# The opening of a fused decoder step: states and gate blocks in turn, and an expert loop whose next gate steps run before the combinations

## Chip, core and metric

The kernel runs on one core of one Trainium2 chip. The metric is the device time of one execution in microseconds (us), and smaller is better. TensorE is called PE here, VectorE DVE, ScalarE ACT, GpSimd POOL and SyncE SP.

## What is computed

One layer of a decoder for 256 prompt tokens and 8 sample tokens (264 in all), width 1024, all in float32. Cut to what matters:

```python
h = rmsnorm(x, g_mix); z = h @ w_in              # w_in is 1024 x 7168
q, f, v, g, u, gate_a, gate_b = split(z)
o, S_new = hgrn2(q, 1 - f, v, log f, S0)         # 8 heads of 128x128; the 8 samples carry a state each:
#   S = f * S0 + k (outer) v                     #   one step of it for a sample
merged = sigmoid(gate_a) * rmsnorm(o) * silu(g) + sigmoid(gate_b) * pool_mixer(u)
x = x + merged @ w_out
# experts: top 4 of 32 for each token
gate = min(h2 @ w_gate[e] + b_gate[e], 7); up = clip(h2 @ w_up[e] + b_up[e], -7, 7)
x = x + weight * (((up + 1) * gate * sigmoid(1.702 * gate)) @ w_down[e] + b_down[e])
x = x + sigmoid(rmsnorm(x) @ w_ple_gate) * (p @ w_ple_proj)
y = rmsnorm(x)
```

The outputs are y, the new states and the new pooling rows. Each of the 32 experts has three weight matrices of 4 MB, 384 MB in all, each read once.

## The kernel before

**The front.** The columns of w_in are loaded by SP in 14 chunks of 512 columns (L423) into four slots; the load of a chunk waits for the last use of the slot. PE turns the rows of x (L645), multiplies all chunks block by block (a block is 8 matmuls, `turned_blocks`, L703), and writes each block into a PSUM bank that it may use again only once ACT or DVE have drained the block before it there. The order is q and f (L741), v, the product of the sample queries with the old states (L764), eight blocks of the output gate g (`gT`, banks 0 to 3 twice), four blocks of gate_a (`gaT`, the same banks), scores, and so on. Beside this ACT and DVE make the new states of the eight samples. For a sample b ACT issues a DMA that spreads the sample's values over all partitions (`spread_values`, L1423, 512 KB, into one of three buffers), and multiplies the old state by f (`decay`, L1428, 8 instructions); DVE adds k times v (`new_state`, L1737, 8 instructions), and POOL stores the new state. A gate block is drained by a sigmoid on ACT (L1405) and a product on DVE (L1705). Both engines do four samples, then gate blocks 0 to 3, then four samples, then gate blocks 4 to 7. Later the pooled rows are multiplied by w_pool (`ypT`, L870), the merged rows by w_out (L891, L915), and the router chooses experts.

**The weights of the experts.** They come in granules of 1 MB, `at_` by number: a pair of experts takes 24 granules, 8 each for gate, up and down (two experts in turn). A step of a product (`products`, L1135) uses two granules, one for each expert: 8 matmuls of 512 columns. There are 16 places in a ring (`gran`) and three more places for single granules at the start (`early`). SP issues the loads in order; each waits until the counter `s_used` has reached a number. In the front the counter comes to 8 at the first `ypT` matmul, to 12 at the first matmul by w_out, to 18 at the turning of the last tile of x (L933); after that it rises by one for each granule used. `load_first` (L439, L437 for `early`) loads the first two pairs, `load_experts` (L445) the others.

**The expert loop.** `pair` handles two experts, 16 pairs in all; the first two are written out. On PE a pair is: four bias matmuls, four gate steps, four up steps, gathering of the first half of the next pair's rows (L1043), a wait for the activation that DVE makes (L2005, L2011), turning it (L1061), four down steps, gathering of the second half (L1043, L1053), and then the combinations (`mix`, L1190) that put the results back into the tokens' rows. In pair 0 PE also turns the router weights (L1000), and multiplies the down biases (L1012, L1020) and turns the embeddings (L1029) between its up steps.

Of the kernel before, what the change touches and what calls it, by code (L numbers as in the profile page):

```python
# [14 lines left out]
P = 128  # L15
# [94 lines left out]
def build(nc, x_prompt, x_sample, p_prompt, p_sample, state_hgrn, state_pool, g_mix, w_in,  # L110
# [14 lines left out]
    with ExitStack() as ctx:  # L125
# [61 lines left out]
        def heads(start):  # L187
# [36 lines left out]
        early = {0: view(TMP, GRAN).rearrange("p (j n) -> p j n", j=2),  # L224
                 1: view(V + D, GRAN).rearrange("p (j n) -> p j n", j=2),
# [183 lines left out]
        def place_of(at_):  # L409
            return (at_ + 1) % RING if at_ <= 17 else at_ % RING  # L410
# [5 lines left out]
        def _(sp):  # L416
# [217 lines left out]
        def _(pe):  # L634
# [88 lines left out]
            pe.wait_ge(s_const, 1)  # L723
            for t, half in ((0, 0), (0, 1), (1, 0), (1, 1), (2, 0)):
                pe.wait_ge(s_rows, t + 1)
                turn_half_rows("hT", htok, t, half)
                if (t, half) == (0, 0):
# [3 lines left out]
                    fill_done(pe.transpose(bank[7][:, 0:32], lgin[0:32, :], ident[0:32, 0:32]), ("lb",))  # L731
            wait_turned("hT")
# [344 lines left out]
            def pair(i0, n, opening=False, last=False, project_tiles=False):  # L1077
# [3 lines left out]
                def granules(m, g):  # L1081

                    for one in range(2):
# [4 lines left out]
                        elif isinstance(i0, int) and i0 == 0:  # L1088
                            place = place_of(at_)
                            pe.wait_ge(s_gr[place], 16 if at_ <= 17 else 16 * ((at_ - 19) // RING + 2))  # L1090
# [5 lines left out]
                def products(m, out, src, first):  # L1096

                    for g in range(4):
# [47 lines left out]
                pe.wait_ge(s_esel, i + 1)  # L1146
# [4 lines left out]
                else:  # L1151
                    pe.wait_ge(s_xe, 2 * i + 1)
                    pe.wait_ge(s_free23, i + 1)
                for r in range(4):
                    rows = slice(r * NE, (r + 1) * NE)
                    pe.matmul((GATE + UP)[r][:, :], esel[rows], bias_gu[rows], start=True, stop=False,  # L1156
                              tile_position=(r * NE, 0))
                if opening:
                    pe.wait_ge(s_xe, 1)
                for m, (out, done) in enumerate(((GATE, s_gate), (UP, s_up))):  # L1160
                    products(m, out, xT_e, False).then_inc(done, 1)
# [4 lines left out]
                else:  # L1166
                    if opening:
                        wait_drained(pe, ("pT", 1))
                    pe.wait_ge(s_oh, i + 2)
                    gather(range(4), s_used)  # L1170
                pe.wait_ge(s_actr, i + 1)
                pe.wait_ge(s_free45, i + 1)
                if project_tiles:
                    wait_drained(pe, ("pp", 1, 1))
                for c in range(2):
# [7 lines left out]
                if not last:  # L1183
                    gather(range(4, KD), s_used)
                    gather_samples()
# [27 lines left out]
                else:  # L1213
                    pe.wait_ge(s_ys, 2 * i + 2)
                    mix(0)
# [80 lines left out]
            pair(0, 1)  # L1296
# [6 lines left out]
            with pe.If(more > 0):  # L1303
# [4 lines left out]
                with pe.Fori(1, NBLK) as b:  # L1308
                    with pe.Fori(0, PAIRS // PER) as q:
                        for n in range(PER):  # L1310
                            pair(b * PAIRS + PER * q, n)
# [10 lines left out]
        def _(act):  # L1322
# [820 lines left out]
```

## Time and profile before

| what | value |
| --- | --- |
| time, median of 3 runs | 1289.98 us (1287.83 to 1291.11) |
| the profiled execution: its own time | 1288.42 us |
| its span from the first to the last instruction | 1286.7 us |
| PE busy | 1213.5 us, 94% |
| DVE, ACT, POOL busy | 339.9, 170.2, 48.6 us |
| moved by DMA | 460.98 MB, mean 358 GB/s over the span |
| mean granted TensorE clock | 0.995 |

The measured time is 1.7 us longer than the span. PE's busy time counts instructions, and in the expert loop the time in which one waits for its operand is partly hidden in the gaps between them, so 94% is not a statement of what bounds the kernel.

### The profile page before, as it was taken

How to read it: one execution, taken by the hardware profiler on the slowest of the kernel's cores; microseconds unless marked ns; L12 is line 12 of the kernel's file. 1: busy time of each engine (PE TensorE's matmuls, PEld its weight loads, DVE VectorE, ACT ScalarE, POOL GpSimd, SP SyncE). 2: the span in 40 equal slices, each digit the busy share in tenths (PEclk: the TensorE clock that was granted, in tenths of full speed). 3: DMA queues.
4: the chain of work that ended last, by engine and by line, in shares of the span. 5: the costliest groups of instructions: out<-in, count | busy, mean ns of one | idle time of the engine just before them, and what ended most of it. 6: DMA issues, size and time to landing. Idle time of an engine off the chain costs nothing.

```text
span 1286.7 us, 15777 instructions
## 1 busy us (share of the span) xinstructions
PE 1213.5 (94%) x6296; PEld 597.6 (46%) x6296; DVE 339.9 (26%) x685; ACT 170.2 (13%) x434; POOL 48.6 (4%) x129
## 2 busy tenths in 40 slices
PE   7999899999999999999898998989898989899996
PEld 6857788856333343333334243333333333434244
DVE  3154434534312222112121121211121212112224
ACT  3135113111100100001010000000010101001013
POOL 2221100010000000000000000000000000000001
PEclk9999999999999999999999999999999999999999
DMA  9847621497989999999999999999999999999971
GB/s 342 285 144 243 243 107 47 180 381 300 418 356 423 421 420 422 422 422 423 422 422 421 422 421 423 422 422 422 422 422 422 422 422 422 422 421 421 422 287 36
DMA packets 79782, 460.98 MB, mean 358 GB/s; under 512 B 8158, under 2 KB 9235, under 8 KB 30842
## 3 DMA queue, kind: packets, MB, share of 16 engines
q1 hardware_dynamic: 74512, 445.18, 84.7%
q0 software_dynamic: 3280, 10.75, 2.6%
q10 hardware_dynamic: 1946, 4.43, 1.0%
q8 instruction: 31, 0.51, 0.2%
q14 instruction: 13, 0.11, 0.0%
HBM read 454.41 MB, written 6.39 MB: 358 GB/s over the span
## 4 chain that ended last, share of the span: by engine, by line
PE 73%; DMA 23%; DVE 3%; issue 1%; SPq 0%; ACT 0%; POOLq 0%; POOL 0%; DVEq 0%; ACTq 0%
PE bank L1135 37%; DMA arena<-in_w_down_dram 19%; PE bank L703 7%; PE bank L1190 5%; PE bank L741 4%; PE bank L1043 3%; DMA arena<-in_w_up_dram 2%; PE bank L684 2%; DMA arena<-sample_values 1%; PE bank L1053 1%; PE bank L1245 1%; PE bank L1156 1%; DVE arena L1737 1%; PE bank L1263 1%; PE bank L891 1%; PE bank L915 1%
## 5 line engine op out<-in xcount | busy, mean ns | idle before, releaser
L1135 PE MATMUL bank<-arena 128*64 128x512 f32 x3072 | 677.1, 595 | 37.0 <-DMA arena<-in_w_up_dram 25.1
L1135 PEld LDWEIGHTS bank<-arena 128*64 128x64 f32 x3072 | 221.4, 137 | 474.1 <-issue 468.9
L703 PE MATMUL bank<-arena 128*128 128x264 f32 x512 | 117.9, 391 | 6.7 <-DVE arena L1705 6.7
L703 PEld LDWEIGHTS bank<-arena 128*128 128x128 f32 x512 | 97.7, 193 | 24.6 <-issue 7.6
L2023 DVE TENSOR_TENSOR arena<-bank,arena 128x512 f32<-128x512 f32 (+1 forms) x92 | 59.0, 682 | 73.2 <-PE bank L1190 72.8
L1190 PE MATMUL bank<-arena 128*128 128x512 f32 (+1 forms) x192 | 75.0, 602 | 0.0
L1043 PEld LDWEIGHTS bank<-arena 128*128 128x128 f32 x512 | 62.7, 196 | 25.4 <-issue 25.2
L2005 DVE TENSOR_SCALAR arena<-bank 128x512 f32<-128x512 f32 x32 | 20.6, 685 | 196.8 <-PE bank L1135 196.8
L2016 DVE COPY arena<-bank 128x512 f32<-128x512 f32 x16 | 11.1, 692 | 230.8 <-PE bank L1135 230.8
L1043 PE MATMUL bank<-arena 128*128 128x128 f32 x512 | 68.8, 288 | 0.0
L1987 DVE TENSOR_SCALAR arena<-bank 128x512 f32<-128x512 f32 x32 | 20.6, 686 | 178.5 <-PE bank L1135 178.5
L741 PE MATMUL bank<-arena 128*128 128x264 f32 x256 | 57.2, 386 | 0.6 <-DVE arena L1659 0.6
L1512 ACT ACTIVATE arena<-arena 128x1024 f32<-128x1024 f32 x16 | 16.9, 1057 | 281.1 <-DVE arena L1987 281.1
L741 PEld LDWEIGHTS bank<-arena 128*128 128x128 f32 x256 | 48.6, 190 | 8.9 <-ACT arena L1378 0.7
L1190 PEld LDWEIGHTS bank<-arena 128*128 128x128 f32 (+1 forms) x192 | 24.5, 155 | 37.4 <-issue 34.9
L1524 ACT ACTIVATE arena<-bank 128x264 f32<-128x264 f32 x16 | 6.3, 391 | 249.5 <-PE bank L1179 249.5
L1500 ACT ACTIVATE arena<-bank,arena 128x128 f32<-128x128 f32 x120 | 32.6, 383 | 39.0 <-PE bank L1053 39.0
L1530 ACT ACTIVATE arena<-bank 128x512 f32<-128x512 f32 x15 | 9.0, 598 | 217.9 <-PE bank L1135 217.9
L614 POOL TENSOR_SCALAR arena<-arena 128x1 f32<-128x1 f32 (+1 forms) x3 | 0.7, 218 | 947.7 <-ACT arena L1552 947.7
L1061 PE MATMUL bank<-arena 128*128 128x128 f32 x128 | 19.6, 296 | 11.5 <-DVE arena L2011 11.5
L684 PE MATMUL bank<-arena 128*128 128x512 f32 x64 | 28.0, 595 | 0.0
L1325 ACT ACTIVATE arena<-bank 128x264 f32<-128x264 f32 (+3 forms) x27 | 12.5, 477 | 107.4 <-PE bank L703 30.6
(258 smaller groups left out, 715.9 us busy)
## 6 DMA issues: line engine op xcount, KB each, us to landing
arena<-in_w_gate_dram SPq DMA_DIRECT2D x128, 1024.0 KB, 26.5
arena<-in_w_up_dram SPq DMA_DIRECT2D x128, 1024.0 KB, 26.7
arena<-in_w_down_dram SPq DMA_DIRECT2D x126, 1024.0 KB, 26.2
arena<-in_w_in_dram SPq DMA_DIRECT2D x14, 2048.0 KB, 10.2
out_dram<-arena POOLq DMA_DIRECT2D x9, 512.0 KB, 8.1
arena<-in_state_hgrn_dram POOLq DMA_DIRECT2D x8, 512.0 KB, 8.7
arena<-sample_values ACTq DMA_DIRECT2D x8, 512.0 KB, 8.1
arena<-in_w_out_dram SPq DMA_DIRECT2D x4, 1024.0 KB, 8.8
```

What stands on the lines that cost most here:

```text
L684: ins = pe.matmul(job_bank(name)[:, :], hT[:, k, toks(t)], w[:, k, :], start=(k == 0), stop=(k == KD - 1))
L703: ins = pe.matmul(job_bank(name)[:, 0:T], w[:, k, (c % 4) * P:(c % 4 + 1) * P], hT[:, k, :], start=(k == 0), stop=(k == KD - 1))
L741: ins = pe.matmul(job_bank((kind, h))[:, 0:T], w_slot[c % NSLOT][:, k, (h % 4) * P:(h % 4 + 1) * P], hT[:, k, :], start=(k == 0), stop=(k ...
L1043: ins = pe.matmul(XG[k // 4][:, (k % 4) * P:(k % 4 + 1) * P], h2[:, t, every_other(k)], oh[:, t, :], start=(k % 4 == 0 and t == 0), stop=F ...
L1061: ins = pe.transpose(out[c][:, j * P:(j + 1) * P], src[:, every_other(k)], ident)
L1135: ins = pe.matmul(out[c][hp(one), :], src[:, k * P + CAP * one:k * P + CAP * one + CAP], w[one][:, j, halves(c)], start=(first and k == 0) ...
L1190: return pe.matmul(out, comb[:, toks(t)], y_sb[:, halves(c)], start=True, stop=True)
L1500: ins = act.activation(xT_e[:, k * P:(k + 1) * P], bank[6 + c][:, (k % 4) * P:(k % 4 + 1) * P], ACT.Copy, scale=gffn[:, k:k + 1])
L1512: act.activation(sig_sb, g_sb, ACT.Sigmoid, scale=ALPHA).then_inc(s_gsig, 1)
L1987: ins = dve.tensor_scalar(g_sb[:, halves(c)], bank[c][:, :], LIMIT, None, ALU.min)
L2005: ins = dve.tensor_scalar(u_sb[:, halves(c)], bank[2 + c][:, :], LIMIT, -LIMIT, ALU.min, ALU.max)
L2023: ins = dve.tensor_tensor(xs, src, xs, ALU.add)
```

## The change

It does two things. In the front, ACT and DVE do one sample and one gate block in turn; the values of the first two samples are spread before the wait for the sample queries' product, and those of sample b+2 after gate block b. PE does 12 matmuls without use before the turning of the rows of x and 3 after it. In the expert loop, PE does the gate biases and three of the four gate steps of the next pair right after the second gathering, ahead of the combinations; the fourth follows after them. The half of the samples' gathering that belongs to the first half moves to it; ACT scales that half before it copies the combination matrix. The down biases and embeddings move from pair 0 to pair 1. The first granules are put into other places, so that the order in which places come free is the order in which granules are used, and the numbers that the loads wait for follow.

```diff
-        early = {0: view(TMP, GRAN).rearrange("p (j n) -> p j n", j=2),
-                 1: view(V + D, GRAN).rearrange("p (j n) -> p j n", j=2),
+        early = {7: view(TMP, GRAN).rearrange("p (j n) -> p j n", j=2),
+                 17: view(V + D, GRAN).rearrange("p (j n) -> p j n", j=2),
                  18: view(HG + 8192, GRAN).rearrange("p (j n) -> p j n", j=2)}
...
         def place_of(at_):
-            return (at_ + 1) % RING if at_ <= 17 else at_ % RING
+            return (at_ + (3 if at_ < 7 else 2)) % RING if at_ <= 16 else at_ % RING
...
-            for at_ in (2, 3, 4, 5, 6, 15, 16, 17):
+            for at_ in (0, 1, 2, 3, 4, 14, 15, 16):
                 load_first(at_, 8)
             sp.wait_ge(s_osq, 1)
-            load_first(0, 8)
+            load_first(7, 8)
             sp.wait_ge(s_ust, 32)
-            load_first(1, 8)
-            for n in range(4):
-                load_first(7 + n, 12)
-            for n in range(4):
-                load_first(11 + n, 18)
+            for at_ in (5, 6, 8, 9):
+                load_first(at_, 12)
+            load_first(17, 12)
+            for at_ in range(10, 14):
+                load_first(at_, 18)
             load_first(18, 18)
             for at_ in range(19, 2 * NGRAN * PER):
-                load_first(at_, at_ + (2 if at_ < 35 else 3))
-                if at_ == 20:
+                load_first(at_, at_ + (0 if at_ < 26 else 1 if at_ < 35 else 3))
+                if at_ == 34:
+                    sp.wait_ge(s_used, 36)
                     sp.dma_start(wproj, ...).then_inc(ld["wproj"], 16)
...
             pe.wait_ge(s_const, 1)
+            for _ in range(12):
+                pe.matmul(bank[6][:, 0:P], ident, ident, start=True, stop=True)
             for t, half in ((0, 0), (0, 1), (1, 0), (1, 1), (2, 0)):
...
+            for _ in range(3):
+                pe.matmul(bank[6][:, 0:P], ident, ident, start=True, stop=True)
             wait_turned("hT")
...
-                        if opening and m == 1 and g == 1:
+                        if second and m == 1 and g == 0:
+                            pe.wait_ge(s_free45, i + 1)
+                            pe.wait_ge(s_free6, i + 1)
                             down_biases()
-                        if opening and m == 1 and g == 2:
+                        if second and m == 1 and g == 2:
                             sample_down_biases()
-                        if opening and m == 1 and g == 3:
+                        if second and m == 1 and g == 3:
                             turn_embeddings()
...
+                def next_gate_steps():
+
+                    biases(range(2), i + 2)
+                    for g in range(3):
+                        if g != 1:
+                            pe.wait_ge(s_xe, 2 * i + 3 + g // 2)
+                        w = list(granules(0, g, n + 1))
+                        for j in range(2):
+                            k = 2 * g + j
+                            for c in range(2):
+                                for one in range(2):
+                                    ins = pe.matmul(GATE[c][hp(one), :],
+                                                    xT_e[:, k * P + CAP * one:k * P + CAP * one + CAP],
+                                                    w[one][:, j, halves(c)], start=False, stop=False)
+                                    if j == 1 and c == 1:
+                                        ins.then_inc(s_used, 1)
...
-                for m, (out, done) in enumerate(((GATE, s_gate), (UP, s_up))):
-                    products(m, out, xT_e, False).then_inc(done, 1)
+                products(0, GATE, xT_e, False, range(0 if opening or alone else 3, 4)).then_inc(s_gate, 1)
+                if not (opening or alone):
+                    pe.wait_ge(s_free23, i + 1)
+                    biases(range(2, 4), i + 1)
+                products(1, UP, xT_e, False).then_inc(s_up, 1)
...
                     gather(range(4), s_used)
+                    gather_samples((0,))
...
                     gather(range(4, KD), s_used)
-                    gather_samples()
+                    gather_samples((1,))
...
                     pe.wait_ge(s_ys, 2 * i + 2)
+                    if not alone:
+                        next_gate_steps()
                     mix(0)
                     mix(1)
...
+            act.wait_ge(s_vrows, 16)
+            for b in range(2):
+                spread_values(b)
             wait_filled(act, ("os",))
-            for n in range(2):
-                for b in range(4 * n, 4 * n + 4):
-                    if b == 0:
-                        act.wait_ge(s_vrows, 16)
-                        for m in range(3):
-                            spread_values(m)
-                    elif b > 2:
-                        act.wait_ge(s_snew, b - 2)
-                        spread_values(b)
-                    decay(b)
-                gate_blocks(range(4 * n, 4 * n + 4))
+            spread_values(2)
+            for b in range(NS):
+                decay(b)
+                gate_blocks([b])
+                if 1 <= b <= NS - 3:
+                    act.wait_ge(s_snew, b)
+                    spread_values(b + 2)
...
+                if not last:
+                    rows_in(i + 1, 0)
                 act.wait_ge(s_cT, i + 1)
                 act.activation(comb, bank[7][:, 0:T], ACT.Copy).then_inc(s_c, 1)
...
-                    rows_in(i + 1, 0)
                     rows_in(i + 1, 1)
...
-            for n in range(2):
-                for b in range(4 * n, 4 * n + 4):
-                    new_state(b)
-                gate_blocks(range(4 * n, 4 * n + 4))
+            for b in range(NS):
+                new_state(b)
+                gate_blocks([b])
```

On DVE the additions of the down biases to x move from pair 0 to pair 1 as well, and ACT copies the turned embeddings there; both engines write pair 1 out ahead of their loops.

## Rows read from the trace of the kernel before

**Rows 1.** The page: rate of all DMA in 40 equal slices of the span

```profile
GB/s 342 285 144 243 243 107 47 180 381 300 418 356 423 421 420 422 422 422 423 422 422 421 422 421 423 422 422 422 422 422 422 422 422 422 422 421 421 422 287 36
```

**Rows 2.** The chain that ended last: start us, us, what

```profile
122.58 11.52 DMA arena<-sample_values
...
162.54 14.24 PE bank L703 x64
...
481.53 27.67 PE bank L1135 x128
...
536.26 27.67 PE bank L1135 x128
...
611.07 26.85 DMA arena<-in_w_down_dram
...
1088.32 26.91 DMA arena<-in_w_down_dram
...
1187.63 28.26 DMA arena<-in_w_up_dram
```

**Rows 3.** Timeline of PE from 84 to 165 us: start, us, instructions [idle before]

```profile
105.40 14.51 PE L703 MATMUL bank<-arena 128*128 128x264 f32 x64
122.00 14.48 PE L703 MATMUL bank<-arena 128*128 128x264 f32 x64 [2.09 <-DVE arena L1705]
141.07 15.99 PE L703 MATMUL bank<-arena 128*128 128x264 f32 x64 [4.59 <-DVE arena L1705]
156.89 3.73 PE L782 MATMUL bank<-arena 128*128 128x128 f32 x32
```

**Rows 4.** Timeline of ACT in the same stretch

```profile
105.51 1.95 ACTq L1423 DMA_DIRECT2D arena<-sample_values  x3
...
133.75 2.45 ACT L1428 ACTIVATE arena<-arena 128x128 f32<-128x128 f32 x8 [4.29 <-DVE arena L1737]
136.10 0.92 ACT L1405 ACTIVATE arena<-bank 128x264 f32<-128x264 f32 x3
```

**Rows 5.** Timeline of DVE in the same stretch

```profile
112.74 8.65 DVE L1737 SCALAR_TENSOR_TENSOR arena<-arena 128x128 f32<-128x128 f32 x32 [4.57 <-DMA arena<-sample_values]
121.42 1.45 DVE L1705 TENSOR_TENSOR arena<-bank,arena 128x264 f32<-128x264 f32 x4
131.16 2.19 DVE L1737 SCALAR_TENSOR_TENSOR arena<-arena 128x128 f32<-128x128 f32 x8 [8.29 <-DMA arena<-sample_values]
```

**Rows 6.** Timeline of ACT in the first 15 us: the scaling of the turned rows

```profile
9.64 2.18 ACT L1378 ACTIVATE arena<-bank,arena 128x128 f32<-128x128 f32 x8 [1.93 <-DVE arena L1650]
```

**Rows 7.** Timeline of PE there: its first product

```profile
12.48 0.68 PE L741 MATMUL bank<-arena 128*128 128x264 f32 x2 [0.63 <-DVE arena L1659]
```

**Rows 8.** Stretches of 5 us: busy of each engine, PE clock, DMA share, GB/s

```profile
310.00:315.00 5.00, 5.00 (x26) 1.57 (x22) 0.00 (x0) 0.00 (x0) 0.00 (x0) 1.00 0.25 107
315.00:320.00 5.00, 5.00 (x32) 3.85 (x32) 1.22 (x3) 0.00 (x0) 0.00 (x0) 1.00 0.69 252
...
370.00:375.00 5.00, 5.00 (x27) 1.43 (x28) 3.67 (x6) 0.00 (x0) 0.00 (x0) 1.00 0.59 247
375.00:380.00 5.00, 5.00 (x26) 1.72 (x24) 0.00 (x0) 0.00 (x0) 0.00 (x0) 1.00 0.64 249
```

**Rows 9.** Timeline of SP's queue, 200 to 460 us: issues of granules

```profile
315.45 0.80 SPq L439 DMA_DIRECT2D arena<-in_w_down_dram  x2
...
345.34 18.70 SPq L439 DMA_DIRECT2D arena<-in_w_up_dram  x8
375.67 11.49 SPq L439 DMA_DIRECT2D arena<-in_w_down_dram  x8
```

**Rows 10.** Timeline of PE in pair 0, and the combinations that end it

```profile
308.34 7.09 PE L1135 MATMUL bank<-arena 128*64 128x512 f32 x32
...
340.18 1.11 PE L1029 MATMUL bank<-arena 128*128 128x128 f32 x6
...
366.33 4.66 PE L1190 MATMUL bank<-arena 128*128 128x512 f32 x12
```

More of the change, by code:

```diff
@@ L1075, in project, with pair, granules @@
                             fill_done(ins, ("pp" + r, t, j))
-            def pair(i0, n, opening=False, last=False, project_tiles=False):
+            def pair(i0, n, opening=False, second=False, last=False, project_tiles=False, alone=False):
                 i = i0 + n
-                def granules(m, g):
+                def granules(m, g, n=n):
                     for one in range(2):
@@ L1094, in granules, with products @@
                             yield gran[at_ % RING]
-                def products(m, out, src, first):
-                    for g in range(4):
+                def products(m, out, src, first, steps=range(4)):
+                    for g in steps:
                         if m == 2 and g % 2 == 0:
@@ L1143, in products, with biases @@
                     return ins
-                pe.wait_ge(s_esel, i + 1)
+                def biases(rs, n_esel):
+                    pe.wait_ge(s_esel, n_esel)
+                    for r in rs:
+                        rows = slice(r * NE, (r + 1) * NE)
+                        pe.matmul((GATE + UP)[r][:, :], esel[rows], bias_gu[rows], start=True, stop=False,
+                                  tile_position=(r * NE, 0))
+                def next_gate_steps():
[13 more added lines that the diff above has]
+                                        ins.then_inc(s_used, 1)
                 if opening:
@@ L1150, in pair @@
                     pe.wait_ge(ld["bias"], 64)
-                else:
+                    biases(range(4), i + 1)
+                    pe.wait_ge(s_xe, 1)
+                elif alone:
                     pe.wait_ge(s_xe, 2 * i + 1)
                     pe.wait_ge(s_free23, i + 1)
[L1154 to L1159, printed above, removed]
-                for m, (out, done) in enumerate(((GATE, s_gate), (UP, s_up))):
-                    products(m, out, xT_e, False).then_inc(done, 1)
+                    biases(range(4), i + 1)
+                products(0, GATE, xT_e, False, range(0 if opening or alone else 3, 4)).then_inc(s_gate, 1)
[3 more added lines that the diff above has]
+                products(1, UP, xT_e, False).then_inc(s_up, 1)
                 pe.wait_ge(s_free6, i + 1)
@@ L1166, in pair @@
                 else:
-                    if opening:
+                    if second:
                         wait_drained(pe, ("pT", 1))
@@ L1174, in pair @@
                     wait_drained(pe, ("pp", 1, 1))
+                if second:
+                    wait_drained(pe, ("bd2", 1))
                 for c in range(2):
@@ L1295, in _ @@
             pair(0, 0, opening=True)
-            pair(0, 1)
+            pair(0, 1, second=True)
             with pe.Fori(1, PAIRS // PER - 1) as q:
@@ L1310, in _ @@
                         for n in range(PER):
-                            pair(b * PAIRS + PER * q, n)
+                            pair(b * PAIRS + PER * q, n, alone=True)
                 pe.wait_ge(s_xe, 2 * NBLK * PAIRS + 2)
@@ L1506, in projected, with pair @@
                 copy_out(name, pps[t][lanes(t), cols(t, n)], piece(name))
-            def pair(i, first=False, last=False, project_tiles=False):
+            def pair(i, first=False, second=False, last=False, project_tiles=False):
                 if first:
@@ L1512, in pair @@
                 act.activation(sig_sb, g_sb, ACT.Sigmoid, scale=ALPHA).then_inc(s_gsig, 1)
-                if first:
+                if second:
                     for k in range(2):
@@ L1595, in _ @@
             pair(0, first=True)
-            with act.Fori(1, PAIRS - PER) as i:
+            pair(1, second=True)
+            with act.Fori(2, PAIRS - PER) as i:
                 pair(i)
@@ L1975, in _, with pair @@
                                  wdn.unsqueeze(2).to_broadcast([P, NT, NBLK, NE])))
-            def pair(i, first=False, last=False):
+            def pair(i, first=False, second=False, last=False):
                 if first:
@@ L2106, in _ @@
             pair(0, first=True)
-            with dve.Fori(1, PAIRS - 1) as i:
+            pair(1, second=True)
+            with dve.Fori(2, PAIRS - 1) as i:
                 pair(i)
```

12 lines of the change are left out of this document (7 added, 5 removed).

## The prediction

> **What bounds the kernel now.** I read the page first. From the tenth slice on the DMA moves 418 to 423 GB/s in every slice but one, until near the end [rows 1]. So I asked the chain of waits whether PE or the transfers set the pace of the expert loop. Between the starts of pieces of PE's products in neighbouring pairs lie 536.26 - 481.53 = 54.73 us [rows 2]: that is a pair for which PE waits for nothing. From 611 us on the chain instead goes through the landing of a down granule in each pair; the first such landing shown is at 637.92 us, the last at 1115.23 us, eight pairs later, so 59.66 us for a pair [rows 2]. Divided by 24 granules that is 2.486 us a granule, or 422 GB/s (1.0486 MB each), the slices' rate. PE thus has 4.9 us in hand in every pair, and uses up in the first pairs the lead of granules with which it began. The last up granule lands at 1187.63 + 28.26 = 1215.89 us [rows 2]; the 70.8 us from there to the end of the span are the same work after the change. The reader is to see that the end is set by one sum: when the stream of granules starts, plus the granules, plus every gap in the stream. PE's work in the loop is not in it.
>
> The stream starts when PE reaches the first pooling product (the counter's 8), so whatever PE loses in the front counts in full. Then I looked for gaps. In the front, PE waits 2.09 us and 4.59 us for DVE's draining of gate blocks, and its third group of four blocks takes 15.99 us, the second 14.48 us [rows 3]. In the stream, the stretches of 5 us show DMA at 107 and 252 GB/s from 310 to 320 us, and at 247 and 249 GB/s from 370 to 380 us [rows 8]; each hole ends with an issue that waited for the counter, at 315.45 us and at 375.67 us [rows 9]. After 380 us there is none.
>
> **The front.** From the first gate block to the scores PE needs 156.89 - 105.40 = 51.49 us [rows 3] for three groups of 64 instructions. One without a wait takes 14.24 us [rows 2], three 42.72 us. So 8.8 us are to be had: 6.7 us of waits, 1.75 us because the group after the 4.59 us of idleness begins slowly, and small change.
>
> Are they had? In turn, one sample and one block cost ACT 2.45 us for the decay, 0.92 / 3 = 0.31 us for the sigmoid [rows 4] and about 0.33 us for an issue, 3.1 us together; DVE 8.65 / 4 = 2.2 us for a state and 1.45 / 4 = 0.36 us for a product [rows 5], 2.5 us. PE takes 14.24 / 4 = 3.56 us for a block. Both drainers are faster, and a bank is wanted again only four blocks later. Sigmoids follow decays without a table load between them [rows 4], so the alternation costs ACT nothing more. What can be late are the spread values. Now three are issued from 105.51 us, and the first is there at 112.74 us [rows 4, 5]; the first two will go some 2 us sooner. The slowest on the chain takes 11.5 us [rows 2], and DVE stood 8.29 us for it [rows 5]. Laid out with 7.2 us for every spread, each issued when its buffer is free, the last state is ready near 137 us, while PE wants its bank only at 105.4 + 11 x 3.56 = 144.6 us. With 11.5 us for every spread from the fourth on, the seventh block drains at 142.9 us, wanted at 141.0 us: 1.9 us lost. I take 8.8 us, with 6.9 us as the other end. The Trainium skill (DMA: Bandwidth & Descriptors, Issuing engines are not separate DMA queues) says that transfers started by any engine run on the same DMA engines and interleave; the 8.29 us of waiting agree, and by that rule the stores and the w_in chunk, now squeezed into less time, would give the slow end, 1.9 us worse.
>
> The 15 matmuls without use: ACT scales the turned rows from 9.64 to 11.82 us, having waited for DVE and not for PE [rows 6]; PE's first product starts at 12.48 us [rows 7]. So at most 0.66 us can come of quicker turning. Twelve such products at twice the 0.23 us of row L782 [rows 3] last 5.6 us, begun when the constants stand, and could reach into PE's first real work by some 0.5 us. Value taken: a gain of 0.5 us (ends: 0.66 gained, 0.5 lost). Front together: 9.3 us.
>
> **The ramp of the stream.** All times here are on the old clock; the front's gain shifts them alike. Nothing changes up to the five granules that the counter's 18 frees: before and after, 14 granules are issued ahead of it. DMA runs out of them at about 311.3 us (107 of 422 GB/s in 5 us). Two granules issued at 315.45 us start moving at 320 - 5 x 252 / 422 = 317.0 us [rows 8, 9], 1.6 us after the issue. Hole: 5.7 us. The second hole is 2.1 + 2.0 = 4.1 us, and about 0.3 us lie between. Sum 10.1 us.
>
> After the change granule 19 takes the place of granule 0, not of the third one used. A step of PE takes 3.5 us (7.09 us for two) [rows 10], so 19 and 20 are issued at 308.4 + 3.5 = 311.9 us and move from 313.5 us: hole 2.2 us. 21 and 22 follow at 315.4 us; after the gathering 23 and 24 at 323.2 us, while DMA, done at 323.4 us, moves again at 324.8 us: 1.4 us. Granule 25 goes at 326.7, 26 and 27 at 331.1 us, moving at 332.7 us: hole 0.2 us. From there PE frees two granules per 3.5 us while DMA takes 5.0 us for two, since the three pieces like the 1.11 us one [rows 10] no longer stand between the up steps (3.1 us, now in pair 1). The long pause in the issues, 364.0 to 375.67 us [rows 9], came of gathering, 4.66 us of combinations [rows 10] and biases ahead of the next gate step. Now down steps end near 360.1 us, the gathering takes 2.7 us and two biases 0.5 us, and the first early gate step frees granules at 366.7 us. They move from 368.3 us, and DMA still has work until 369.8 us (the 1 MB of w_ple_proj included, which is only moved). The hole is gone, with 1.5 us over; the thinnest place after it is granule 56 in pair 1, where 0.9 us are left. New holes: 2.2 + 1.4 + 0.2 = 3.8 us. Gain 10.1 - 3.8 = 6.3 us. Ends: 9 us if the small holes close as well, 3 us if each thin place falls short by 1 to 2 us.
>
> The row above gives 1.6 us from issue to first byte. The Trainium skill (DMA: Bandwidth & Descriptors, Anatomy of one DMA) puts the fixed part of a transfer at about 2.0 us, measured on GpSimd's path; by that each of the three new holes would be 0.4 us longer, and the whole gain 1.2 us smaller.
>
> **The loop behind the ramp.** ACT's scaling of half the rows ahead of its copy, the split gathering (some 0.6 us less for PE) and the early gate steps all lie in PE's 4.9 us of slack; priced at nothing. Without that cover they would still not add work: a pair is the same instructions. At the end the combinations (4.66 us) and biases (0.5 us) now lie behind three gate steps and not before them. PE idles 5.0 - 3.5 = 1.5 us in each step that waits for DMA; five steps are left until the last up granule, 7.5 us against 5.2 us. So it still waits for that granule, by some 2 us. Cost nothing; the bound is 1 to 2 us.
>
> **Sum.** 8.8 + 0.5 + 6.3 = 15.6 us. The profiled execution took 1288.4 us (span 1286.7 us), which gives 1272.8 us (span 1271.1 us). The median of the three runs is 1.6 us above it, the lowest 0.6 us below; I put the forecast at 1273.5 us.
>
> **Rivals.**
> - *The holes only move* (0.10). The later issue of one of the thin places, or down biases that hold pair 1 up, opens a hole of 4 us. For it: margins of 0.9 and 1.5 us. Against: after 380 us no hole shows now. Time about 1278 us.
> - *The front gives back* (0.10). Spreads come late or a wait appears between 157 and 298 us. Against: PE runs without a wait there, with DVE and ACT following it. Time 1275 us with slow spreads, up to 1282 us if everything is lost.
> - *More than summed* (0.07): every hole closes, 1269 to 1270 us.
> - *PE becomes the bound, slower* (0.04). PE would stand before the early gate steps for ACT's scaled rows or DVE's expert selector, with the combinations, and thus DVE's freeing of banks, queued behind. It decides once a pair costs PE more than 59.66 us, 5.5 us above what I sum; to end 4 us above the time before it must reach (15.6 + 4) / 15 = 1.3 us beyond that, near 61 us a pair. For it: the order is longer and each wait holds more. Against: all those signals come while PE still does down steps. Time 1294 us or more.
> - *The change does nothing for the end* (0.03): the last landing stays where it is because DMA moves granules more slowly when it starts sooner. Nothing shows that. 1288 to 1290 us.
> - My forecast (0.66): 1270 to 1276 us.
>
> With 0.3% (3.9 us) as what a measurement here can tell, that makes faster 0.93, same 0.03, slower 0.04. The range reaches to the first two rivals: 1269 to 1281 us.
>
> **What the profile after would show.** Gate blocks on PE back to back, scores near 148 us, and full clock there. First expert granule issued near 245 us rather than 254.5. The stretches with DMA under 400 GB/s after that together some 6 us shorter. Pairs still 59.66 us in the long part, with landings of granules on the chain. The last up granule near 1200 us. I am wrong if the chain in the middle runs through PE alone, if waits for spread values stay, or if a hole of over 2 us appears after the second pair's start.

## The result and the profile after

The change takes the time from 1290.06 to 1275.64 us (medians of 4 runs each), ratio 0.9901, 95% interval 0.9874 to 0.9928. Forecast were 1273.5 us and a range of 1269 to 1281 us. The profiled execution after has a span of 1273.0 us, 13.7 us less than before; the sum had said 15.6 us.

I read the profile after in the order of the prediction's steps, and keep an account with three marks: PE's first expert step, its last down step of pair 13 (the last one at which DMA sets the pace in both kernels), and the end of its last up step in pair 15. From the first mark to the second I call the way the ramp, from the second to the third the tail. The page's rates in 40 slices first:

```profile
GB/s 347 287 143 261 273 67 97 238 354 355 417 409 415 422 421 422 420 422 421 422 422 422 422 422 422 422 422 422 422 421 422 422 422 422 422 422 420 421 241 36
```

Slice 10 now has 355 GB/s, slice 12 has 409 instead of 356 [rows 1]. The chain that ended last, in the front and at the end:

```profile
11.87 57.20 PE bank L746 x256
...
104.86 42.92 PE bank L704 x192
147.78 3.57 PE bank L787 x32
...
226.98 1.90 PE bank L646 x16
...
297.47 7.02 PE bank L1142 x32
...
349.04 2.08 PE bank L1048 x16
...
353.12 10.45 PE bank L1172 x48
...
1088.16 26.34 DMA arena<-in_w_gate_dram
1114.50 0.14 issue
1114.64 3.65 PE bank L1172 x16
```

The twelve blocks run in one piece of 42.92 us where three had stretched over 51.49 us [rows 3]. PE's first product starts at 11.87 us, not 12.48 us [rows 7]. The turning of the output rows (L646) takes 1.90 us; in the kernel before it took 3.54 us, with the granted clock at the lower of its two levels. The first expert step starts at 297.40 us against 308.34 us [rows 10]: 10.9 us earlier, forecast 9.3 us. Behind the landing of a gate granule of pair 14 at 1114.50 us the chain holds no transfer at all, unlike before, where the last up granule stands in it [rows 2].

The last up granule landed at 1198.95 us, 16.9 us earlier than before, and the end came only 13.7 us earlier: here the end no longer follows the landing. Of the 16.9 us, 10.9 lie ahead of the first expert step and 4.7 in the ramp. The last 1.4 us lie behind the start of the last down step of pair 13: from there to the landing it is 99.2 us, and 99.2 to 100.0 us in every kernel below with early steps ahead of the combinations in all pairs, 100.2 to 100.7 us in the others.

DVE in the front (start, us, instructions, idle before):

```profile
128.49 2.19 DVE L1774 SCALAR_TENSOR_TENSOR arena<-arena 128x128 f32<-128x128 f32 x8 [3.70 <-DMA arena<-sample_values]
...
135.95 2.19 DVE L1774 SCALAR_TENSOR_TENSOR arena<-arena 128x128 f32<-128x128 f32 x8 [1.62 <-DMA arena<-sample_values]
138.06 0.43 DVE L1742 TENSOR_TENSOR arena<-bank,arena 128x264 f32<-128x264 f32 x1
```

It still waits for spread values, 3.70 us at most instead of 8.29 us [rows 5], and the last state is ready at 138.1 us (laid out: near 137 us). PE wants that bank at about 144 us, so no wait reaches it.

The stretches of 5 us in which the stream has holes, and SP's issues beside them:

```profile
280.00:285.00 5.00, 5.00 (x13) 2.29 (x12) 2.26 (x13) 0.00 (x0) 0.00 (x0) 1.00 0.72 300
285.00:290.00 5.00, 4.90 (x31) 3.87 (x30) 2.42 (x6) 2.72 (x5) 0.20 (x1) 1.00 0.52 180
...
300.00:305.00 5.00, 5.00 (x27) 1.86 (x23) 0.00 (x0) 0.00 (x0) 0.00 (x0) 1.00 0.62 224
...
310.00:315.00 5.00, 5.00 (x26) 1.73 (x24) 0.00 (x0) 0.00 (x0) 0.00 (x0) 1.00 0.79 303
...
375.00:380.00 5.00, 5.00 (x26) 1.65 (x24) 2.85 (x5) 0.00 (x0) 0.00 (x0) 1.00 1.00 378
```

```profile
301.08 11.62 SPq L439 DMA_DIRECT2D arena<-in_w_down_dram  x5
...
342.24 7.63 SPq L439 DMA_DIRECT2D arena<-in_w_up_dram  x5
356.73 18.30 SPq L439 DMA_DIRECT2D arena<-in_w_down_dram  x8
```

With 423 GB/s as full rate, 224 GB/s for 5 us is a hole of 2.4 us (laid out: 2.2 us), 303 is one of 1.4 us (1.4 us). The pause between the up and down issues is now 356.73 - 349.87 = 6.9 us long, 11.6 us before [rows 9], and no hole follows it. What is left are dips of 0.2 to 0.5 us, as at 375 us. (A hole is counted here as what a stretch lacks to 423 GB/s, put as time.) From the first expert step to the last down step of pair 13 it is 807.03 us before and 802.33 us after: the ramp gives 4.7 us, forecast 6.3 us.

Last, PE in the later pairs and at the end. Before:

```profile
613.21 3.65 PE L1135 MATMUL bank<-arena 128*64 128x512 f32 x16 [1.42 <-DMA arena<-in_w_up_dram]
...
1115.37 3.65 PE L1135 MATMUL bank<-arena 128*64 128x512 f32 x16 [1.31 <-DMA arena<-in_w_down_dram]
...
1216.03 3.65 PE L1135 MATMUL bank<-arena 128*64 128x512 f32 x16 [0.94 <-DMA arena<-in_w_up_dram]
1219.61 1.05 PE L1072 MATMUL bank<-arena 128*8 128x256 f32 x16
```

After:

```profile
781.68 3.65 PE L1142 MATMUL bank<-arena 128*64 128x512 f32 x16 [1.31 <-DMA arena<-in_w_up_dram]
...
1099.73 3.65 PE L1142 MATMUL bank<-arena 128*64 128x512 f32 x16 [1.03 <-DMA arena<-in_w_down_dram]
...
1191.85 13.96 PE L1142 MATMUL bank<-arena 128*64 128x512 f32 x64
1205.73 1.05 PE L1077 MATMUL bank<-arena 128*8 128x256 f32 x16
```

Past 430 us, the first wait of PE for a granule that the timeline shows comes at 613 us before and at 782 us after: PE uses up its lead more slowly. Before, PE waits 0.94 us for the last up granule; after, its four up steps are one piece of 13.96 us without a wait. From the down step to the end of the up steps it takes 106.00 us instead of 104.24 us. The account: 10.9 + 4.7 - 1.8 = 13.8 us, and the spans differ by 13.7 us.

### The profile page after: what moved, and what is told of

It reads as the page before. It is cut to its first block, busy times and chain, and to the rows that moved or that the text cites. A ratio compares the mean times of both kernels' runs of the same rounds, so it can differ in the third digit from the quotient of the medians.

```text
span 1273.0 us, 15848 instructions
## 1 busy us (share of the span) xinstructions
PE 1242.8 (98%) x6326; PEld 614.1 (48%) x6326; DVE 340.0 (27%) x685; ACT 172.5 (14%) x434; POOL 48.6 (4%) x129
## 4 chain that ended last, share of the span: by engine, by line
PE 78%; DMA 15%; SPq 5%; DVE 1%; issue 1%; ACT 0%; POOLq 0%; POOL 0%; DVEq 0%
PE bank L1142 29%; DMA arena<-in_w_gate_dram 10%; PE bank L1172 9%; PE bank L704 9%; PE bank L1224 5%; SPq L445 5%; PE bank L746 4%; PE bank L1048 3%; PE bank L685 2%; DMA arena<-in_w_down_dram 2%; DMA arena<-in_w_up_dram 2%; PE bank L1158 2%; PE bank L1058 2%; PE bank L1281 1%; PE bank L1299 1%; PE bank L896 1%
## 5 line engine op out<-in xcount | busy, mean ns | idle before, releaser
L1142 PEld LDWEIGHTS bank<-arena 128*64 128x64 f32 x2352 | 166.3, 137 | 349.3 <-issue 347.8
L1172 PEld LDWEIGHTS bank<-arena 128*64 128x64 f32 x720 | 51.1, 137 | 107.1 <-issue 107.1
L2043 DVE TENSOR_SCALAR arena<-bank 128x512 f32<-128x512 f32 x32 | 20.6, 686 | 193.3 <-PE bank L1142 193.3
L1048 PE MATMUL bank<-arena 128*128 128x128 f32 x512 | 68.9, 288 | 0.0
L1547 ACT ACTIVATE arena<-arena 128x1024 f32<-128x1024 f32 x16 | 16.9, 1057 | 298.0 <-DVE arena L2023 298.0
L1158 PE MATMUL bank<-arena 32*128 32x512 f32 x128 | 40.4, 627 | 0.0
L1058 PE MATMUL bank<-arena 8*128 8x128 f32 x256 | 38.6, 290 | 0.0
L1058 PEld LDWEIGHTS bank<-arena 8*128 8x128 f32 x256 | 32.5, 191 | 3.8
```

What stands on the lines that cost most here:

```text
L1048: ins = pe.matmul(XG[k // 4][:, (k % 4) * P:(k % 4 + 1) * P], h2[:, t, every_other(k)], oh[:, t, :], start=(k % 4 == 0 and t == 0), stop=F ...
L1058: ins = pe.matmul(XG[c][:, k * P:(k + 1) * P], h2[rows, 2, every_other(4 * c + k)], oh[rows, 2, :], start=False, stop=True, skip_group_che ...
L1142: ins = pe.matmul(out[c][hp(one), :], src[:, k * P + CAP * one:k * P + CAP * one + CAP], w[one][:, j, halves(c)], start=(first and k == 0) ...
L1172: ins = pe.matmul(GATE[c][hp(one), :], xT_e[:, k * P + CAP * one:k * P + CAP * one + CAP], w[one][:, j, halves(c)], start=False, stop=False)
```

## The experiments

"Ramp" is the time from the first expert step to the start of the last down step of pair 13, "tail" from there to the end of the last up step, "pair" the distance of two pairs near 500 us, where PE waits for nothing; all in us, from one profiled execution of each kernel. Ratios are to the kernel before, run beside each.

| kernel | first step | ramp | tail | pair | ratio, 95% interval |
| --- | --- | --- | --- | --- | --- |
| before | 308.34 | 807.03 | 104.24 | 54.73 | |
| changed | 297.40 | 802.33 | 106.00 | 56.27 | 0.9901 (0.9874 to 0.9928) |
| changed, again | 297.68 | 802.82 | 106.01 | 56.27 | 0.9880 (0.9861 to 0.9900) |
| front only | 297.39 | 806.99 | 104.21 | 54.74 | 0.9927 (0.9900 to 0.9954) |
| turns only | 298.37 | 806.93 | 104.17 | 54.73 | 0.9920 (0.9891 to 0.9948) |
| loop only | 305.55 | 802.90 | 106.01 | 56.27 | 0.9963 (0.9934 to 0.9992) |
| order only | 310.51 | 807.29 | 103.92 | 54.74 | 0.9991 (0.9969 to 1.0012) |
| old places | 302.03 | 803.16 | 106.00 | 56.27 | 0.9889 (0.9846 to 0.9931) |
| no early steps | 300.40 | 803.56 | 104.43 | 54.73 | 0.9891 (0.9848 to 0.9934) |
| combinations first | 300.53 | 803.86 | 105.71 | 56.32 | 0.9907 (0.9889 to 0.9926) |
| places one by one | 299.24 | 801.25 | 105.99 | 56.27 | 0.9884 (0.9866 to 0.9902) |
| projection in pair 8 | 297.44 | 803.39 | 103.23 | 56.26 | 0.9891 (0.9871 to 0.9912) |
| splits | 306.97 | 808.14 | 105.71 | 56.32 | 1.0020 (0.9998 to 1.0042) |
| early steps in two pairs | 297.80 | 802.54 | 104.45 | 54.73 | 0.9878 (0.9845 to 0.9910) |

**The front, whole and in part.** The first is the kernel before with the front's hunks of the diff and nothing of the loop; the second leaves out these as well:

```diff
-            for _ in range(12):
-                pe.matmul(bank[6][:, 0:P], ident, ident, start=True, stop=True)
...
-            for _ in range(3):
-                pe.matmul(bank[6][:, 0:P], ident, ident, start=True, stop=True)
```

> Only the front's part of the change: states and gate blocks in turn, early spreads, the 15 matmuls without use; expert loop and order of granules as before. If the end is one sum of stream start, granules and holes, the whole shift of the front arrives: the first expert product 9.3 to 11 us earlier and the same shift at the end, a ratio near 0.992. If something in the ramp or at the end takes the front's gain back, the shift at the end is less than half of that at the first expert product.

> Only states and gate blocks in turn, without the 15 matmuls without use. The blocks on PE run without a wait, 8.7 us saved there; PE's first product stays where it was, within 0.1 us of 12.48 us. If the slow-clock stretch at the turning of the output rows (236 us before) depends on what PE did since the 140 us stretch, it is gone here too and the first expert product comes 10.3 us earlier; if it was the matmuls at the start that removed it, it stays, and the shift is 8.7 us.

The front's shift, 10.95 us at the first expert step, arrives in full: ramp and tail of the front-only kernel are those of before within 0.05 us. In the turns-only kernel the blocks take 42.92 us as well, and PE's first product stands at 12.84 us. In the front-only kernel it stands at 11.86 us. With the matmuls without use it started between 11.86 and 12.28 us in nine profiled executions, without them between 12.48 and 13.14 us in five: 0.8 us on average, laid out as 0.5 us. The expectation's "within 0.1 us of 12.48 us" was too narrow. The turning of the output rows took 1.90 us in both kernels.

The 1.6 us that the turning saved are not the change's, though: it took 1.90 us also in the loop-only, order-only and splits kernels, which have the old front, and 3.49 and 2.83 us in two kernels with the changed front (places one by one, old places). Where the lower clock falls differs from one execution to the next. Over the four profiled executions with the old front the first expert step starts at 307.8 us on average, over the ten with the new one at 298.8 us: 9.0 us, beside a forecast of 9.3 us.

**The loop alone, and the order of the granules alone.** All hunks but the front's; and only the three hunks with `early`, `place_of` and the loads (with the number at which PE's wait changes over).

> Only the loop's part: gate steps ahead of the combinations, down biases in pair 1, new order of granules; front as before. Sum of the stream: the landing of the down granules in the long stretch comes about 4.7 us earlier than before, and PE, which in the full change runs without a wait through the last two pairs, gives back about 1.8 us at the end: 3 us faster, ratio near 0.998. Rival, parts add up without the loss at the end: 4.7 us faster. Rival, the loop part only pays after the shorter front: no gain.

> The kernel before with only the new order of the granules in their places and the new counter values. The hole at the first expert step shrinks by 3.5 us. If holes add up, the end comes about 4 us earlier. If the stream is pinned again by the late first gate step of pair 1, behind the combinations, the time won is given back in the hole there, which grows by the same amount: landings from the second pair on, and the end, as before within 0.5 us, ratio 1.000.

The loop part gives 4.1 us in the ramp (4.7 us expected) and loses 1.8 us in the tail, as expected. The order alone gives nothing, as expected too, but not in the way expected. Counted from the first expert step, its granules 19 and 24 land 3.6 and 6.1 us earlier than before, granule 34 only 2.5 us earlier, and granule 35 at the same time (55.7 us in both). From granule 35 on the loads are issued when they were before. The time is given back in small dips ahead of it, the hole before granule 40 does not grow:

```profile
325.00:330.00 5.00, 5.00 (x46) 1.74 (x43) 1.04 (x2) 0.30 (x1) 0.00 (x0) 1.00 0.82 300
...
355.00:360.00 5.00, 5.00 (x26) 1.61 (x24) 0.00 (x0) 0.00 (x0) 0.00 (x0) 1.00 0.87 314
...
375.00:380.00 5.00, 5.00 (x26) 1.72 (x24) 1.12 (x2) 0.00 (x0) 0.00 (x0) 1.00 0.30 70
```

70 GB/s for 5 us are a hole of 4.2 us; the 247 and 249 GB/s of the kernel before [rows 8] are 4.1 us together.

**Old places in the changed kernel.** The reverse of the order-only kernel.

> The changed kernel with the old places of the granules and the old counter values. The first hole of the stream is 5.7 us again and nothing later gives it back as it did in the kernel before, since the pause at granule 40 is gone: 1.5 to 2.3 us more than the changed kernel from the first expert step to the last down step of pair 13, 804 to 804.6 us. If the places were worth nothing here too, as they were alone, 802.3 us.

The ramp is 803.16 us, 0.3 to 0.8 us above the changed kernel's two, where 1.5 us or more were expected. The direction is right, the size is not. Counted from the first expert step, granule 24 lands 6.2 us later than in the changed kernel, granules 40 and 56 only 2.5 and 1.4 us later, and granule 96 within 0.2 us: step by step the changed kernel gives the places' gain back, 1.1 us of it in dips between 375 and 405 us that this kernel does not have (0.1 us in sum, beside 1.2 to 1.3 us). Its first step stood 4.6 us later than the changed kernel's, because of two stretches of low clock, one of them (2.9 us) between the start of the stream and that step. That does not show in the ramp: in the two kernels below that have the same delay and the new places, granule 20 lands 10.9 us after the first step, as in the changed kernel.

**Where early steps are needed.** Without them (`ahead` is False in every pair):

```diff
+                    if ahead:
                         next_gate_steps()
...
-                    gather_samples((1,))
+                    gather_samples((1,) if ahead else range(2))
```

> The changed kernel without any early gate steps: pairs as before, unsplit, but front, places and the moved down biases and embeddings (3.1 us out of pair 0) as changed. Sum of the stream: the first gate step of pair 1 comes 3.1 us earlier than before, 5.5 us later than with early steps; hole at granule 40 of 2.5 to 3.7 us. From the first expert step to the last down step of pair 13 it takes 804 to 805 us, between before (807.0) and changed (802.3). Rival, early steps alone make the gain: 807 us.

And with them, but behind the combinations:

```diff
-                    next_gate_steps()
                     mix(0)
                     mix(1)
                     pe.wait_ge(s_xe, 2 * i + 3)
                     mix(2)
+                    next_gate_steps()
```

> The changed kernel with the combinations again ahead of the biases and three gate steps in every pair, all else kept. The sum of the stream: at the fortieth granule the issue waits for the first gate step of pair 1, 4.6 us later than in the changed kernel, of which 1.5 to 2 us were spare: a hole of 2.6 to 3 us there. The down landings in the long stretch are 2.6 us later than in the changed kernel. At the end PE has its combinations done while it waits for gate granules, so it loses nothing there: the end only about 1 us later. Rival, early gate steps matter in every pair: over 4 us slower.

Without early steps the ramp is 803.56 us (804 to 805 us expected), so 3.5 of the 4.7 us come with the three pieces of 1.1 us moved out of pair 0 and the new places. From the first expert step to the end of the last up step this kernel takes 807.99 us, the changed kernel 808.33 and 808.83 us: early steps in every pair, with the splits that they bring, gain nothing over none that these marks show. Both profiled executions here had some 7 us of low clock ahead of their first step, which stands 3.0 us later for it. With the combinations first the ramp is 803.86 us, 1.0 to 1.5 us above the changed kernel; the hole before granule 40 is 3.9 us (192 and 321 GB/s), but the dips behind it, 1.2 to 1.3 us in sum in the changed kernel (375 to 405 us), are gone. My expectation that the tail would be saved in this kernel failed: 105.71 us. Its median is 1279.05 us, 4.8 us above that of the changed kernel beside it, which is the size that the rival had named. In the profiled pair ramp and tail together account for only 0.7 us of that and the late first step for 2.9 us; whether this is so in the other executions no trace shows.

**Places given free one by one.**

```diff
+                    elif half == 1 and k % 2:
+                        ins.then_inc(s_used, 1)
...
-            for at_ in range(10, 14):
-                load_first(at_, 18)
+            for at_ in range(10, 14):
+                load_first(at_, (13, 14, 15, 18)[at_ - 10])
```

> The changed kernel, with the four places under w_out given free one by one in the last product by it instead of together behind it, so that three loads are issued 2 to 6 us earlier. The hole of 4.3 us in the stream near 283 to 288 us closes. If holes add up, the end comes up to 4 us earlier. If the next loads are pinned by PE's first expert step, the hole only moves to behind granule 18, and landings from granule 19 on and the end stay the same within 0.5 us.

```profile
285.00:290.00 5.00, 4.90 (x23) 2.94 (x21) 1.64 (x3) 1.15 (x2) 0.00 (x0) 1.00 1.02 423
...
295.00:300.00 5.00, 5.00 (x38) 3.54 (x38) 3.39 (x13) 0.00 (x0) 0.00 (x0) 1.00 0.54 226
300.00:305.00 5.00, 5.00 (x26) 1.71 (x24) 0.51 (x3) 0.00 (x0) 0.00 (x0) 1.00 0.18 39
```

The first hole is closed (423 GB/s), and a hole of 2.3 + 4.5 us stands around PE's first step at 299.24 us. The holes from 280 to 425 us sum to 9.9 us, in the changed kernel to 10.0 and 9.7 us: it only moved. Counted from the first step, granules 20, 24 and 40 land when they do in the changed kernel, within 0.2 us. From granule 48 on they come about 1 us sooner, and the ramp is 1.1 to 1.6 us shorter, though the loads up to granule 59 are issued at the same times; why is open. Differences of 1 us between ramps should thus not be read closely. The end is the same (1275.35 beside 1274.30 us).

**What binds the tail.** My first theory was the projection of the embeddings:

> The changed kernel with the projection of the embeddings (four pieces of 1.9 us on PE, 7.6 us) moved from pair 14 to pair 8, where PE waits for DMA 5 us in every pair. If this projection, with the combinations behind the gate steps, is what makes PE the bound in the last two pairs, PE waits again for the last up granule and the time falls by 1.8 us, ratio near 0.9885. If PE's lateness there comes of something else (DMA's own end, the last pair's form), nothing changes.

```profile
901.94 3.65 PE L1142 MATMUL bank<-arena 128*64 128x512 f32 x16 [0.91 <-DMA arena<-in_w_up_dram]
...
1200.47 3.65 PE L1142 MATMUL bank<-arena 128*64 128x512 f32 x16 [1.33 <-DMA arena<-in_w_up_dram]
...
1216.71 5.80 PE L1142 MATMUL bank<-arena 128*64 128x512 f32 x26 [1.25 <-DMA arena<-in_w_down_dram]
```

PE waits again for the last up granule, so lifting 7.6 us of work out of pair 14 makes it punctual. But it then waits 1.25 us for down granules, and the time does not tell (1276.18 beside 1274.30 us, intervals overlapping), also because its ramp is 0.6 to 1.1 us longer, for a reason that stays open. My expectation was also wrong in that PE waits 5 us in every pair there: in the changed kernel pair 8 is where its first wait stands (782 us), and with the projection in it PE's first wait past 430 us comes at 902 us. This does not say why PE was late in the changed kernel and not in the kernel before, which has the same projection in the same pair.

The combinations-first kernel gave the hint: no early steps before the combinations, yet a long tail and pairs of 56.32 us. Rows of PE for one pair near 540 us, changed kernel (L1158 are bias matmuls, L1058 the samples' gathering):

```profile
540.09 3.65 PE L1142 MATMUL bank<-arena 128*64 128x512 f32 x16
543.67 1.13 PE L1158 MATMUL bank<-arena 32*128 32x512 f32 x4
544.73 13.96 PE L1142 MATMUL bank<-arena 128*64 128x512 f32 x64
...
560.69 1.21 PE L1058 MATMUL bank<-arena 8*128 8x128 f32 x8
...
579.32 0.85 PE L1058 MATMUL bank<-arena 8*128 8x128 f32 x5
...
596.36 3.65 PE L1142 MATMUL bank<-arena 128*64 128x512 f32 x16
```

and before:

```profile
566.63 1.22 PE L1061 MATMUL bank<-arena 128*128 128x128 f32 x8 [0.67 <-DVE arena L2011]
...
584.12 1.21 PE L1053 MATMUL bank<-arena 8*128 8x128 f32 x16
...
589.85 1.14 PE L1156 MATMUL bank<-arena 32*128 32x512 f32 x8
```

Four bias matmuls together (8 records) take 1.14 us, two alone (4 records) 1.13 us. Sixteen records of sample gathering take 1.21 us, eight take 1.21 us too. In the kernel before the trace starts the first records of the four bias matmuls within 0.02 us of each other: they run on top of each other, each on a row group of its own. The changed kernel splits both into halves and pays each half at the price of the whole. A kernel that only splits them, with no other part of the change:

```diff
+                biases(range(2))
...
                 products(0, GATE, xT_e, False)
+                biases(range(2, 4))
...
                     gather(range(4), s_used)
+                    gather_samples((0,))
```

> The kernel before with two edits that add no work: the two bias matmuls for up stand behind the gate steps, and the samples' gathering of the first half stands with the gathering of the first half. No early gate steps, old places. If split matmuls of separate row groups lose their overlap: 56.2 us for a pair when PE waits for nothing instead of 54.7 us, the first expert step to the last down step of pair 13 as before (807 us), and 1.5 to 2 us lost between there and the last up step. Rival, the longer pair of the changed kernel comes of waits around the early gate steps: pairs stay 54.7 us.

Pairs of 56.32 us and a tail of 105.71 us: both as in the changed kernel, with nothing moved ahead of anything. The ramp is 1.1 us longer than before, where none was expected: the load of granule 40 waits for PE, and is issued 1.4 us later after the first step. In the median (ratio 1.0020, interval from 0.9998) the loss is not clear of noise. About 2.2 us more work in a pair, less the 0.67 us of waiting for DVE that the gathering now fills, makes the 1.54 us.

**Early steps only where the ramp needs them.** The changed kernel, with early steps and the two splits in pairs 0 and 1 alone:

```diff
-            pair(0, 0, opening=True)
-            pair(0, 1, second=True)
-            with pe.Fori(1, PAIRS // PER - 1) as q:
+            pair(0, 0, opening=True, ahead=True)
+            pair(0, 1, second=True, begun=True, ahead=True)
+            pair(PER, 0, begun=True)
+            pair(PER, 1)
+            with pe.Fori(2, PAIRS // PER - 1) as q:
```

> The changed kernel with early gate steps and split gathering and biases only at the ends of pairs 0 and 1; from pair 2 on each pair is as in the kernel before. If the order only pays in the ramp, and each later pair is longer because its four bias matmuls and its sample gathering, split in two, no longer overlap (pair of 56.27 us for 54.73 us when PE waits for nothing), then: the last down step of pair 13 starts 802 to 803 us after the first expert step, as in the changed kernel; pairs in which PE waits for nothing take 54.7 us; PE waits again for the last up granule and the stretch from that down step to the last up step's end is 100.7 us as before, not 102.4 us; the end about 1.5 us earlier, ratio near 0.987. Rival, the projection of the embeddings is what binds PE at the end: no change of that stretch.

```profile
1100.34 3.65 PE L1142 MATMUL bank<-arena 128*64 128x512 f32 x16 [1.32 <-DMA arena<-in_w_down_dram]
...
1201.20 3.65 PE L1142 MATMUL bank<-arena 128*64 128x512 f32 x16 [1.15 <-DMA arena<-in_w_up_dram]
1204.79 1.05 PE L1077 MATMUL bank<-arena 128*8 128x256 f32 x16
```

Ramp, pair and tail came as expected (the 100.7 us of the expectation end at the start of the last up step; measured 100.9 us). Its median is 1274.78 us, that of the changed kernel 1275.64 and 1274.30 us: these runs do not tell the 1.5 us apart. What is shown is the pair, the tail and the wait, not a gain in time.

## Why the prediction held, point by point

- *The bound.* Right up to pair 13, and shown there: stream start plus granules plus holes. The parts add up: the front alone leaves ramp and tail untouched, the loop alone gives the ramp of the whole change. It is not right for the end: the last up granule came 16.9 us earlier and the end 13.7 us, since PE is behind when it lands: from the landing to the end of the span it is 74.1 us, not the 70.8 us counted as the same before and after. Landings also stand on the chain in the long stretch only from 790 us on, not from 611 us. The rates of 418 GB/s and more begin with the eleventh slice, not the tenth (300).
- *The front.* Blocks 8.6 us (8.8 laid out), start 0.6 us (0.5). The whole front gave 10.9 us in the profiled pair and 9.0 us over all profiled executions. 1.6 us of the profiled pair come of where a slow stretch fell; that is luck, and it hides as much of what the ramp fell short by. DVE still waits for spreads, which I had named as a sign of being wrong; it costs nothing, since PE never waits for DVE.
- *The ramp.* The holes at granules 19 and 23 and the closed one before 40 came as laid out; the term was 6.3 us and measured 4.7 us. The missing 1.6 us are about the dips between 375 and 405 us (1.2 to 1.3 us) and 0.4 us in the three small holes (4.2 us beside 3.8; by the prediction's own times the third, from 332.3 to 332.7 us, is 0.4 us and not 0.2). One reason is in the rows: gathering and two biases ahead of the early steps were laid out at 2.7 + 0.5 = 3.2 us, and take 353.12 - 349.04 = 4.1 us. The 1.6 us from issue to "first byte" are the time to full rate; the first packets of 8 KB start 0.95 us after the issue. For the holes it is the time to full rate that counts: with 1.6 us they came as laid out within 0.2 us, and not 0.4 us longer each.
- *The loop behind the ramp.* The failing term of the sum, and the failing step. I wrote that a pair "is the same instructions" and priced the order at nothing, with a bound of 1 to 2 us. The instructions are the same, their time is not: 1.54 us a pair more. In the long stretch DMA hides it; PE's slack there is 59.66 - 56.27 = 3.4 us a pair and not 4.9 us. In the last pairs, where the kernel before had 0.94 us in hand, it costs 1.8 us of tail. I had also counted the steps' idle time only from pair 15 on, without the 7.6 us of projection in pair 14.
- *The rivals.* "The holes only move" did not happen to the whole change, but it is what happens to places given free one by one; the order alone gives its gain back in dips. "PE becomes the bound" happened for the last two pairs only.

## What to carry to other kernels

When a ring of buffers feeds a stream at its full rate, write down for each issue what it waits for and when that comes; a hole closed ahead of a later pinned issue gains nothing, so find the last pinned one first. An order that costs PE time and helps only while the ring fills should be confined to the pairs in which it fills. Before calling a move free because no instruction is added, look at whether the rows being separated had run on top of each other, and check the slack in the last iterations, not in the middle ones.

## What was not expected of the hardware

Small matmuls that use separate row groups of the array cost as much in twos as in fours: two bias matmuls of 32 rows by 512 columns take 1.13 us, four 1.14 us; four sample matmuls of 8 rows by 128 columns take 1.21 us, eight on two row groups also 1.21 us.

The granted clock falls to its lower level for stretches of some 3 or 7 us at places that change between executions of the same code. The first expert step, behind the same front, stood at 305.55, 306.97, 308.34 and 310.51 us. In each of the four executions with the old front the blocks behind a wait of 2.4 to 4.6 us for DVE ran at the lower level. The other slow stretches, as at the turning of the output rows or at the router ahead of the first expert step, fell in some executions and not in others, and what sets them stays open.
